# One block for compression and first attention, and a re-dealt first projection, in a fused transformer kernel

## The reference, cut to what matters

```python
proj = jnp.einsum('bsd,dc->bsc', rms_norm(x, norm_gain), w_in)
# compress: blocks of 32 tokens, stride 16, + position, silu(flat @ w1 + b1) @ w2
kc_cmp = rope(rms_norm(compress(kc, cmp_pe_k, w1k, b1k, w2k), kc_gain), cmp_pos)
vc_cmp = compress(vc, cmp_pe_v, w1v, b1v, w2v)
o_nsa = g0 * attend_cmp(qn, kc_cmp, vc_cmp) + g1 * attend_sel(qn, ks, vs) + g2 * attend_win(qn, kw, vw)
o_nsa = o_nsa * silu(z_n)
# dsa: score = sum_h relu(qi_h . ki) * wi_h, the top 128 keys of each row, softmax over them
mixed = concat([o_nsa, attend_dsa(qd, kd, vd, score) * silu(z_d)])
return x + mixed @ w_out
```

## Time and profile before

| what | value |
|---|---|
| three timed runs | 3018.84, 3019.22, 3013.61 us; median 3018.84 us |
| the profiled execution | 3014.08 us, its span 3012.3 us (1.8 us lie around the span) |
| first projection | 23 to 225.5 us of the span |
| `compress` | 225.5 to 253.4 us |
| `attend_first` | 253.4 to 427 us |

### The profile page before, as it was taken

The page is one execution under the profiler, slowest core; times in us unless marked ns, Lnnn a source line. Parts: engine busy times, 40 slices in busy tenths (PEclk is TensorE's granted clock), DMA queues, the critical chain, the costliest instruction groups (busy, mean ns, idle before and its releaser), DMA issues. The chain is left out here.

```text
span 3012.3 us, 43721 instructions
## 1 busy us (share of the span) xinstructions
PE 2911.4 (97%) x16784; PEld 2575.3 (85%) x16784; DVE 2329.1 (77%) x4062; ACT 1125.3 (37%) x1850; POOL 131.0 (4%) x99
## 2 busy tenths in 40 slices
PE   8999989999999999999999999999999999999998
PEld 7786558899999886788999998899999877779997
DVE  6666757798988776657888888798888855578886
ACT  4335545333323423334332234433233423254443
POOL 2331420000000000000000000000000000000000
PEclk9999999999999999999999999999999999999999
DMA  6423032233433241222333333133333230223332
GB/s 198 120 77 103 22 116 88 92 120 119 126 114 110 78 137 36 69 70 68 115 119 119 102 116 92 63 119 119 113 101 120 73 102 10 68 84 99 99 99 91
DMA packets 317538, 292.78 MB, mean 97 GB/s; under 512 B 12562, under 2 KB 269844, under 8 KB 315796
## 3 DMA queue, kind: packets, MB, share of 16 engines
q1 hardware_dynamic: 317332, 289.98, 31.5%
HBM read 284.18 MB, written 2.10 MB: 95 GB/s over the span
## 5 line engine op out<-in xcount | busy, mean ns | idle before, releaser
L2560 PE MATMUL PS<-hid_f,w_hi 128*128 128x512 f32 (+1 forms) x2464 | 563.8, 345 | 6.2 <-DVE hid_f L2776 6.2
L2560 PEld LDWEIGHTS PS<-hid_f,w_hi 128*128 128x128 f32 x2464 | 389.2, 188 | 65.2 <-DVE hid_f L2776 7.6
L2549 PE MATMUL PS<-x_hi_f,w_hi 128*128 128x384 f32 (+1 forms) x1216 | 390.8, 321 | 0.0
L2549 PE MATMUL PS<-x_lo_f,w_hi 128*128 128x384 f32 (+1 forms) x1216 | 390.7, 321 | 0.0
L2549 PE MATMUL PS<-x_hi_f,w_lo 128*128 128x384 f32 (+1 forms) x1216 | 390.6, 321 | 0.0
L2560 PE MATMUL PS<-hid_f,w_lo 128*128 128x512 f32 x1232 | 338.9, 344 | 0.0
L2641 ACT ACTIVATE w_hi<-w_raw 128x512 fp32r<-128x512 f32 (+1 forms) x420 | 244.8, 604 | 203.1 <-DMA w_raw<-in_w_ffn_dram 138.1
L2144 DVE SCALAR_TENSOR_TENSOR ada_product<-ada_w,ada_s 128x1024 f32<-128x1024 f32 x228 | 278.4, 1221 | 28.1 <-DMA ada_w<-in_w_ada_dram 24.2
L2549 PE MATMUL PS<-t_hi_f,w_hi 128*128 128x384 f32 (+1 forms) x912 | 293.3, 322 | 0.0
L2549 PE MATMUL PS<-t_hi_f,w_lo 128*128 128x384 f32 (+1 forms) x912 | 293.0, 321 | 0.0
L2549 PE MATMUL PS<-t_lo_f,w_hi 128*128 128x384 f32 (+1 forms) x912 | 293.0, 321 | 0.0
(11 more groups left out here) (394 smaller groups left out, 5303.7 us busy)
## 6 DMA issues: line engine op xcount, KB each, us to landing
w_raw<-in_w_ffn_dram SPq DMA_DIRECT2D x256, 512.0 KB, 4.6
ada_w<-in_w_ada_dram SPq DMA_DIRECT2D x120, 512.0 KB, 3.5
w_raw<-in_w_in_dram SPq DMA_DIRECT2D x46, 512.0 KB, 5.2
w_raw<-in_w_out_dram SPq DMA_DIRECT2D x24, 512.0 KB, 6.6
ada_s<-in_conditions_dram SPq DMA_DIRECT2D x7, 1024.0 KB, 5.1
ada_room<-in_w_ada_dram SPq DMA_DIRECT2D x14, 512.0 KB, 3.8
q_plain<-in_w_ada_dram SPq DMA_DIRECT2D x10, 512.0 KB, 4.4
w_raw<-in_w_ffn_dram SPq DMA_DIRECT2D x16, 256.0 KB, 2.8
```

What stands on the lines that cost most here:

```text
L2549: last = nc.tensor.matmul(bank_of(kind), wt[:, k, :], xt[:, k0 + k, :], start=(k == 0 and one == 0), stop=(k == 3 and one == 2))
L2560: last = nc.tensor.matmul(ps[:, a:e], wt[:, f, :], hid[:, f, v, a:e], start=(start and f == 0 and one == 0), stop=(end and f == n - 1 and ...
```

## The change

1. In `project_first` ACT takes all four relus of a step ahead of `stack`; before, two stood ahead of it and two behind.
2. The ten `ada` tiles of the projection are dealt `[1, 2, 2, 1, 1, 1, 1, 1]` over the turns, before `[1, 2, 2, 2, 2, 1]`.
3. `compress` becomes a class whose pieces stand in `attend_first`'s queues: one block, no barrier between the two.
4. For t = 3 the units run `sel, win, cmp`; the row products of the first unit stand between the hidden products of the values.
5. The eight top-8 rounds of `compress` move behind the maxima of unit 1; `rounds_at` and the `ada` deal (`ADA_FIRST`) are new; PE keeps warm with 24 passes where it had 40; one of ACT's table loads disappears (silu is taken up in one piece).

```diff
-                ahead = index_items(i - 1)
-                for m in ahead[:2]:
+                for m in index_items(i - 1):
                     relu_of(act, m)
                 stack(i - 3)
-                for m in ahead[2:]:
-                    relu_of(act, m)
...
-    order = [(t, b) for t in (3, 2, 0, 1) for b in (("cmp", "sel", "win", "dsa") if t == 0 else ("cmp", "sel", "win"))]
+    branches = {t: ("sel", "win", "cmp") if t == QT - 1 else ("cmp", "sel", "win") for t in range(QT)}
...
-    rounds_at = [1, 4, 5, 1, 5, 5, 0, 0, 0, 0, 0, 2]
+    rounds_at = [8, 6, 0, 1, 5, 5, 1, 1, 1, 1, 1, 1]
...
-            pe.wait_ge(rounded, 1)
-            row(0, 0)
+            def beside_values(j):
+                if j == 4:
+                    cmp.turn_hidden(pe, 0)
+                if j == 9:
+                    cmp.output(pe, 0)
+                if j % 2:
+                    if j == 1:
+                        pe.wait_ge(rounded, 1)
+                    row(0, j // 2)
+
+            c.keep_warm(12, 6)
+            cmp.hidden(pe, 0)
+            cmp.hidden(pe, 1, beside_values)
             for j in range(units[1].row_items):
                 row(1, j)
-                nc.tensor.matmul(c.PS[:, 4 + j % 2, 0:P], c.ident[:], c.ident[:], start=True, stop=True)
-                if j == 2:
-                    turn(0)
+                nc.tensor.matmul(c.PS[:, 2 + j % 2, 0:P], c.ident[:], c.ident[:], start=True, stop=True)
+                if j == 1:
+                    cmp.turn_hidden(pe, 1)
+                if j == 4:
+                    cmp.output(pe, 1)
+            pe.wait_ge(cmp.made, 1)
+            turn(0)
...
+                if (i, m) == (0, 5):
+                    cmp.wait_made(pe)
+                    row(2, 0)
...
             ch.link(nc.vector.memset(Mx[:], 0.0))
-            for i in range(2):
-                maxes(i)
             for n in range(early):
                 pick(n)
+            maxes(0)
+            cmp.sum_squares(dve)
+            maxes(1, range(4))
+            cmp.values(dve)
+            cmp.norm_keys(dve, ch)
+            maxes(1, range(4, units[1].row_items))
...
+ADA_FIRST = [0, 1, 0, 0, 1, 1, 0, 0, 0, 0, 1, 1, 1, 2, 2, 1]
...
-                         room[:, 7 * D:8 * D], [1, 2, 2, 2, 2, 1], ())
+                         room[:, 7 * D:8 * D], [1, 2, 2, 1, 1, 1, 1, 1], ())
...
-            rest = AdaShare(c.ada, s_c, bufs, room[:, 2], [0, 1, 1, 0, 1, 1, 0, 0, 0, 0, 0, 1, 1, 1, 2, 1], (), share)
```

More of the change, by code:

```diff
@@ L1107, in project_first @@
     ring.ahead = False
[L1110 to L1130, removed]
-        room = c.hT.rearrange("p k n -> p (k n)")
[L1132 to L1215, removed]
-                for i in range(2):
[L1218 to L1239, removed]
-                act.wait_ge(kturned, 1)
-                nc.scalar.activation(KKc[:].rearrange("p g c -> p (g c)"), c.PS[:, 4, 0:GROUPS * CMP_PAD], ACT.Copy).then_inc(kmoved, 1)
-                move(1)
-            @block.gpsimd
-            def _(pool):
-                nc.gpsimd.memset(G[:, :, :, :, N_CMP:CMP_PAD], 0.0).then_inc(zeroed, 1)
-                pool.wait_ge(zeroed, 1)
-                nc.gpsimd.memset(KLc[HD:HD + 4].bitcast(F32), 1.0).then_inc(zeroed, 1)
-                pool.wait_ge(zeroed, 2)
[L1250 to L1256, removed]
-                    nc.vector.tensor_copy(S[0:HD, i, 1, :], T[HD:P, i, :])
-                    nc.vector.tensor_copy(S[HD:P, i, 1, 0:SEQ - 1], T[HD:P, i, 1:SEQ]).then_inc(shifted, 1)
-                    if i == 0:
-                        dve.wait_ge(zeroed, 1)
-                        dve.wait_ge(small_in, 64)
-                    dve.wait_ge(stacked, i + 1)
-                    dve.wait_ge(shifted, i + 1)
-                    for g in range(GROUPS):
-                        for part in range(2):
-                            src = S[:, i, g, part * CMP_STRIDE:part * CMP_STRIDE + N_CMP * CMP_STRIDE].rearrange(
-                                "p (c j two) -> p j c two", c=N_CMP, two=2)[:, :, :, 0]
-                            js = slice(part * 8, part * 8 + 8)
-                            last = nc.vector.tensor_tensor(G[:, i, js, g, 0:N_CMP], src,
-                                                           pe_t[:, i, js, None].to_broadcast([P, 8, N_CMP]), ALU.add)
-                    last.then_inc(gathered, 1)
-                gather(0)
-                gather(1)
-                topk.rounds(ch, 8)
-                for i in range(len(share.tiles) - 1):
-                    share.vector(dve, ch, i)
-                dve.wait_ge(squared, 1)
-                nc.vector.reduce_sum(ss[:], sq[:], AX_X).then_inc(summed, 1)
-                dve.wait_ge(rooted, 1)
-                dve.wait_ge(w2_in, 96)
-                ch.link(nc.vector.reciprocal(inv[:], rt[:]))
-                ch.link(nc.vector.tensor_tensor(kraw[:], kraw[:], inv[:, :, None].to_broadcast([CMP_PAD, GROUPS, HD]), ALU.mult))
-                ch.link(nc.vector.tensor_tensor(kraw[:], kraw[:], gain[:, None, :].to_broadcast([CMP_PAD, GROUPS, HD]), ALU.mult))
-                nc.vector.tensor_tensor(A[:], kraw[:], cos[:, None, :].to_broadcast([CMP_PAD, GROUPS, HD]), ALU.mult)
-                for a in range(2):
-                    lo, hi = a * 32, a * 32 + 32
-                    last = nc.vector.tensor_tensor(B[:, :, lo:hi], kraw[:, :, 32 - lo:64 - lo],
-                                                   sin[:, None, lo:hi].to_broadcast([CMP_PAD, GROUPS, 32]), ALU.mult)
-                ch.link(last)
-                for a in range(2):
-                    last = nc.vector.tensor_tensor(R2[:, :, a, :], A[:], B[:], ALU.add)
-                last.then_inc(normed, 1)
-                share.vector(dve, ch, len(share.tiles) - 1)
-                dve.wait_ge(tabs_in, 16 * len(tabs))
-                dve.wait_ge(zeroed, 3)
-                dve.wait_ge(kmoved, 1)
-                ch.link(nc.vector.tensor_tensor(KLc[0:HD].rearrange("p g c -> p (g c)"), c.PS[0:HD, 4, 0:GROUPS * CMP_PAD],
-                                                KKc[0:HD].rearrange("p g c -> p (g c)").bitcast(F32), ALU.subtract))
-                dve.wait_ge(out_done, 2)
-                ch.link(nc.vector.tensor_scalar(Vc[0:CMP_PAD, :, 0:HD], c.PS[0:CMP_PAD, 5, 0:GROUPS * HD].rearrange("p (g d) -> p g d", g=GROUPS),
-                                                valid[:], None, ALU.mult))
@@ L1319, in __init__, with attend_first @@
         self.row_items = HEADS // self.per_row
-def attend_first(c, sb, rows, O, Q, KK, KL, KKc, KLc, Vx, Vc, topk, tri, tabs, gates, dram, share):
+def attend_first(c, sb, cmp, rows, O, Q, KK, KL, KKc, KLc, Vx, Vc, topk, tri, tabs, gates, dram, share):
     nc = c.nc
-    order = [(t, b) for t in (3, 2, 0, 1) for b in (("cmp", "sel", "win", "dsa") if t == 0 else ("cmp", "sel", "win"))]
-    units = [FirstUnit(t, b) for t, b in order + [(t, "dsa") for t in range(1, QT)]]
+    branches = {t: ("sel", "win", "cmp") if t == QT - 1 else ("cmp", "sel", "win") for t in range(QT)}
+    units = [FirstUnit(t, b, n) for t in (3, 2, 0, 1) for n, b in enumerate(branches[t] + (("dsa",) if t == 0 else ()))]
+    units += [FirstUnit(t, "dsa", 3) for t in range(1, QT)]
+    tabs_in = c.tally("cmp_tabs_in").sem
     n_units = len(units)
-    rounds_at = [1, 4, 5, 1, 5, 5, 0, 0, 0, 0, 0, 2]
+    rounds_at = [8, 6, 0, 1, 5, 5, 1, 1, 1, 1, 1, 1]
     sc_at = topk.at
@@ L1371, in _ @@
         def _(sp):
+            cmp.load(sp)
+            for dst, name in zip(tabs, ("neg_eye", "cmp_neg")):
+                sp.dma_start(dst[:], dram[name]).then_inc(tabs_in, 16)
+            cmp.load_more(sp)
+            share.ada.load_small(sp)
+            share.load_conditions(sp)
+            sp.wait_ge(cmp.hid_done, 1)
             ring = Ring(c)
             ring.load_ahead(sp, c.step, cols_step(ring, dram["w_out"], ALL_TILES))
+            sp.wait_ge(cmp.hid_done, 2)
             for i in range(n_units):
@@ L1453, in back @@
                     pe.wait_ge(finished, i)
+                else:
+                    cmp.wait_made(pe)
                 pe.wait_ge(moved, min(i + 4, n_units))
@@ L1473, in _ @@
                     turn(t)
-                if i == 0:
-                    for j in range(m * 4, m * 4 + 4):
-                        row(2, j)
+                if (i, m) == (0, 1):
+                    pe.wait_ge(moved, 2)
+                    cmp.turn_keys(pe)
+                if (i, m) == (0, 5):
+                    cmp.wait_made(pe)
+                    row(2, 0)
                 if i + 3 < n_units:
@@ L1517, in keep @@
                 nc.scalar.activation(OT[:, g, :], c.PS[0:66, 4 + g, :], ACT.Copy).then_inc(kept, 1)
+            cmp.stack(act, 0)
+            cmp.stack(act, 1)
             nc.scalar.activation(identr[:], c.ident[:], ACT.Copy)
             nc.scalar.activation(trir[:], tri, ACT.Copy)
+            act.wait_ge(tabs_in, 32)
             nc.scalar.activation(cnegr[:], cneg[:], ACT.Copy).then_inc(rounded, 1)
             copy_q(0)
```

(26 more changed lines are left out.)

187 lines of the change are left out of this document (178 added, 9 removed).

## The result

The changed kernel takes 3038.13 us (median of 4, 3037.84 to 3040.02) against 3017.40 (median of 4): 1.0071 times as long, 95% interval 1.0055 to 1.0086. It is 20.7 us slower. The forecast was no change, with 3025 as the upper end. The profiled execution took 3040.0 us, the slowest of the four; its span is 3038.2, 25.9 us more than before. What follows cuts up these 25.9 us, not the 20.7 of the medians.

The account below looks back on a forecast made before the run. TensorE was taken to bound the projection, with VectorE equal to it in part of attention. Terms -4.0 + 5.8 - 3.3 + 1.0 = -0.5 us gave 3018 us on the median's basis, range 3014 to 3022 (8 in 10: 3008.5 to 3025).

Parts of the forecast that it names:

- slower rival: Projection and attention: 1.7 us of clock lost behind all four other new waits, sum +6.3, 3025.1 us; chance 0.20.
- low clock from 266 us: Start of attention: a low clock after TensorE stood 5.4 and 3.3 us first eats VectorE's 2.0 us wait; counted 0.
- The relus' order: Projection, turns 7 and 9: stacking copies behind the last relu delay squares and TensorE's means; +5.8 us, bounds 0 and +7.
- The tiles: Projection: moving turn 4's second `ada` tile ends a 3.5 us wait, a shorter one for squares follows; -4.0 us (-5.2 to -2.6).
- exclusive lock of the port pair: Projection: by this rule the removed tile frees GpSimd's three operations at once, squares are in time; tiles term -5.2 us.
- The start of attention: Block start to first score: hidden products 1.1 us earlier, but the root waits behind silus; first score +2.7 us (+1.0 to +4.5).
- The units behind it: Attention units after the first score: the late start is paid back; -3.3 us from hidden products on, the +2.7 included.
- the rounds: Units 6 to 11, one top-8 round each: a 2.1 us wait in unit 10 less 1.1 for `chosen`; +1.0 us (0 to +3).
- The forecast wait of 2.0 us near 298: Attention, behind unit 2: TensorE waits 2.0 us for maxima queued behind an `ada` tile and rounds on VectorE.
- the rival of the free relus: Projection: the new relu order costs nothing, as copies find another gap or index scores run later; 3013.3 us, chance 0.06.

## Why the prediction was wrong

**The step that failed is the clock.** The slower rival had the mechanism of "each new wait drops the clock" and the price of 1.7 us a fall from the earlier trace rows. The falls cost 6.8, 1.7, 12.0 and 5.1 us, and the largest isn't the price of a wait: it comes from two light units side by side, and 10.2 of its 12.0 us stayed when the stop ahead was gone. The prediction looked at the new order of units for its waits and never at what the products of neighbouring units use of the array. The earlier trace rows gave the price of falls in heavy work only. The sentence on the low clock from 266 us, which "would first eat those 2.0 us" and was put at 0, failed too: filling the two stops gained 4.9 us by the medians and 6.4 between the first hidden product and the last output.

**The relus' order** (+5.8 forecast): right in mechanism, place and size; measured +7.4 alone and 6.5 when taken back. The wait is 3.05 us where 3.3 was forecast, 1.7 us of clock are lost behind it (121 to 130 us), and the wait of turn 9 is 0.70 for 0.8. In the trace with this change alone the block starts 6.4 us later, less the 0.6 that it was late at its first means (61.90 against 61.29): 5.8, the forecast.

**The tiles** (-4.0): measured 0. This is the second step that failed. The wait for the squares was 2.40 us, near the bound of 2.6 and not the 1.2 that I took; the clock behind the old wait wasn't saved, since it fell behind the new one too; and in the run with this change alone another 1.7 us lost at 131 to 138 us ate the rest. The result "-5.2" by the exclusive lock of the port pair (the Trainium skill, "SBUF — State Buffer") didn't come: the stacking copies started at 85.70 us, 1.3 us sooner than before once the start of the means at 62.67 against 61.29 is taken off. One tile's 4.3 us gone freed GpSimd by less than a third of that. The lock itself agrees with the rows; what failed is the claim that the tile was all that stood in GpSimd's way. With the tile gone, VectorE's split of the weights (`w_lo`) moved up beside GpSimd's first rotation, where it had stood beside the last. The first row is of the kernel before, where GpSimd's last rotation ran from 82.40 for 3.19 us; the others are of the changed kernel:

```profile
81.10 3.37 DVE L1020 TENSOR_TENSOR w_lo<-w_raw,w_hi 128x2048 fp32r<-128x2048 f32 x1
78.01 3.37 DVE L1017 TENSOR_TENSOR w_lo<-w_raw,w_hi 128x2048 fp32r<-128x2048 f32 x1
79.19 3.34 POOL L921 TENSOR_TENSOR hT<-hT,rot_cos 128x512 f32<-128x512 f32 x1
84.38 1.29 POOL L925 TENSOR_TENSOR hT<-hT 128x512 f32<-128x512 f32 x1
```

In both kernels GpSimd's operation beside the split ends 1.1 to 1.2 us behind the split's end (85.59 and 84.47 before, 82.53 and 81.38 after), and the last one after, with nothing beside it, takes 1.29 us in all.

**The start of attention** (+3.8 from the first hidden product to the first score, that is +2.7 and the 1.1 of an earlier start): measured +5.9 in length, while the hidden products came 2.1 us sooner after their block's start, where I had 1.1. The root's place behind the silus is 3.1 us of it, as the run with the silus moved shows. Mis-sized was the way to the root and not what follows it: the silu of the values began 20.8 us behind the first hidden product (forecast 19.4), the root ended 28.7 us behind it (26.7), and from there to the first score it took 8.2 us (8.2). TensorE stood 4.75 and 2.74 us, less than the 5.4 and 3.3 of the forecast.

```profile
257.28 0.38 ACT L1212 ACTIVATE cmp_hid_rows<-PS 64x256 f32<-64x256 f32 x1 [4.07 <-PE PS L1164]
264.94 0.29 ACT L1230 ACTIVATE cmp_rt<-cmp_ss,eps 32x2 f32<-32x2 f32 x1
267.80 0.79 PE L1389 MATMUL PS<-KK,Q 128*128 128x512 f32 x1 [4.75 <-DVE row_max L1640]
```

The row behind the Trainium skill's "What ACT_TABLE_LOAD costs" ("ScalarE: Activation LUTs") stays as it was: the load takes 1.28 us from 263.64, the root stands at 264.94, with no drain between. The 1.38 us of drain that the Trainium skill gives aren't seen here.

**The units behind it** (-3.3 - 2.7, and +1.0 for the rounds): measured +16.7 in time and 0 at full clock. From the first score to unit 9's turn it took 82.6 us before, 76.6 in the forecast and 94.3 after, 77.6 of it at full clock; behind that turn the forecast has +1.0, and measured are +5.0, or +1.6 at full clock. So the count of the units' work was nearly right. It took all of that work at full clock, where even the kernel before had lost 5.1 us, and that is what failed. The stop at unit 9's turn, said to shrink to tenths, stayed at 3.43 us, since the tile of unit 5 stands ahead of it. The forecast wait of 2.0 us near 298 came at 313, 2.67 us; the one in unit 10 as 2.44 us for 2.1.

Two sums of the prediction were off as well, without effect on the outcome: the bounds of its terms add up to about 3009 and 3025, wider than the 3014 to 3022 given, and the rival of the free relus takes off 5.0 us of a term of 5.8.

What stays open: why the same light units lose 12.0, 10.2 and 5.1 us, why the kernel before lost 5.1 us more when its block was held up by 6.3 us, and why the stop of 3.4 us at unit 9's turn is followed by a loss of 1.7, 3.4, 5.1 or 6.8 us, trace by trace, on the same products. Whether the moment at which the work comes sets this the runs don't show.

## What to carry to other kernels

When an order of units changes, ask what the neighbours are to TensorE: here two units of products on 32 rows or columns side by side cost 12.0 us in clock, more than any wait that the change moved. Read the granted clock in every stretch where TensorE is "busy" before calling it the bound. A queue that puts long copies ahead of something TensorE needs can be late by nearly the whole of them (4.8 of 5.1 us for the squares here, with the new order of relus alone): look at who waits behind, not at who is free.

## What was unexpected of the hardware

TensorE at 22.88 of 23 us busy was granted 0.50; with matmuls of 128 x 128 between, 0.93 over the same units. A fall behind a stop of 3.4 us lost 1.7 us in the kernel before (at 346 us) and 5.1 us in the changed one (at 368), on the same sequence of products. Held up by 6.3 us, the code of before lost 17.1 us in place of 12.0.
